# Two-layer hybrid decoder on 8 cores: attention values and softmax denominators from one full-width matmul

## The reference, cut to what matters

```python
DEPTH, D_MODEL, N_HEADS, KV_HEADS, HEAD_DIM, WINDOW = 2, 2048, 16, 4, 64, 128
def _layer(x, ...):
    z = x @ w_in                       # q 1024, k 256, v 256, conv 3*512, pool 512
    # A: sliding-window attention: query blocks of 128, 256 keys each, 4 query heads per kv head
    s = q @ k^T * HEAD_DIM**-0.5 + bias(distance);  s = -1e30 outside the window
    m = max(max(s), sink)
    a = (exp(s - m) / (sum(exp(s - m)) + exp(sink - m))) @ v
    # B: gated short convolution      c = gb * conv3(gc * h)
    # C: multi-scale causal pooling   pm = (trailing mean - token) @ pool_w * pool_scale
    x = LN(alpha * x + concat(a, c, pm) @ w_o)
    x = LN(alpha * x + (silu(g) * val) @ w_down)   # g, val from conv3(x @ w_up)
```

## Time and profile before

| | us |
|---|---|
| median of 3 runs | 2840.01 |
| all three | 2839.45, 2840.01, 2842.6 |
| the profiled execution, its own time | 2839.04 |
| its span, slowest core (2) | 2837.5 |
| spans of cores 0 to 7 | 2835.9, 2828.8, 2837.5, 2834.1, 2837.0, 2832.3, 2833.8, 2829.4 |
| granted TensorE clock, mean of a core | 0.987 to 0.990 |

### The profile page before, as it was taken

The page is one execution under the profiler, slowest core; times in us unless marked ns, Lnnn a source line. Parts: engine busy times, 40 slices in busy tenths (PEclk is TensorE's granted clock), DMA queues, the critical chain, the costliest instruction groups (busy, mean ns, idle before and its releaser), DMA issues.

```text
span 2837.5 us, 52754 instructions; the slowest of 8 cores (2828.8 to 2837.5 us)
## 1 busy us (share of the span) xinstructions
PE 2729.5 (96%) x18484; PEld 1739.9 (61%) x18484; DVE 1476.1 (52%) x3278; ACT 931.4 (33%) x2005; POOL 496.2 (17%) x755
## 2 busy tenths in 40 slices
PE   7999999999999999999999989999999999999994
PEld 4655666666666666665665556566666666666653
DVE  0375466563555355445616644775535544563546
ACT  1565055330232033113636630643203311330236
POOL 2221063000000000001623102610000000000024
PEclk9999999999999999999999999999999999999997
DMA  9515524434444443443472154344454344434425
GB/s 163 104 31 157 109 49 79 81 77 80 76 74 69 82 75 69 67 89 62 106 192 42 37 157 94 60 75 75 80 88 75 69 68 85 73 61 82 75 46 125
DMA packets 84349, 238.12 MB, mean 84 GB/s; under 512 B 9288, under 2 KB 30032, under 8 KB 83536
## 3 DMA queue, kind: packets, MB, share of 16 engines
q0 software_dynamic: 61136, 190.23, 38.6%
q1 hardware_dynamic: 22944, 44.41, 5.1%
HBM read 405.99 MB, written 21.27 MB: 151 GB/s over the span
## 4 chain that ended last, share of the span: by engine, by line
PE 93%; DVE 2%; ACT 2%; issue 1%; DMA 1%; POOL 1%; DVEq 0%; POOLq 0%; ACTq 0%
PE ps L196 93%; DVE xT L196 1%; DMA X<-xg 1%; ACT xT L196 1%; DVE scr L196 1%; ACT scr L196 0%; POOL xT L196 0%; ACT rstd L196 0%; DMA slab<-w_in 0%; DVE H L196 0%; POOL H L196 0%; DVE rstd L196 0%; ACT ps L196 0%; DVE small L196 0%; DVEq L191 0%
## 5 line engine op out<-in xcount | busy, mean ns | idle before, releaser
L196 PE MATMUL ps<-X,slab 128*128 128x386 bf16 (+3 forms) x10944 | 1681.7, 315 | 21.8 <-DMA slab<-w_in 11.8
L196 PEld LDWEIGHTS ps<-X,slab 128*128 128x128 bf16 x10944 | 1059.4, 97 | 628.1 <-issue 52.2
L196 PE MATMUL ps<-H,slab 128*128 128x384 bf16 (+1 forms) x5760 | 895.5, 314 | 0.0
L196 DVE SCALAR_TENSOR_TENSOR scr<-ps,fcw_s,scr 128x384 f32<-128x384 f32 (+1 forms) x1056 | 616.0, 584 | 410.7 <-ACT scr L196 353.9
L196 PEld LDWEIGHTS ps<-H,slab 128*128 128x128 bf16 x5760 | 561.6, 98 | 307.8 <-issue 7.1
L196 ACT ACTIVATE scr<-ps,fcw_s 128x384 f32<-128x384 f32 (+1 forms) x528 | 291.1, 553 | 1054.9 <-PE ps L196 1054.7
L196 DVE TENSOR_TENSOR xT<-xT,ps 128x384 f32<-128x384 f32 (+1 forms) x549 | 264.5, 521 | 207.8 <-PE ps L196 189.9
L196 POOL DMA_DIRECT2D slab<-w_up x176 | 93.6, 532 | 924.7 <-PE ps L196 924.7
L196 DVE TENSOR_TENSOR H<-scr 128x384 bf16<-128x384 f32 (+3 forms) x278 | 143.4, 518 | 98.1 <-ACT scr L196 69.6
L196 ACT ACTIVATE scr<-xT 128x384 bf16<-128x384 f32 (+1 forms) x192 | 94.5, 496 | 226.0 <-DVE xT L196 181.9
L196 DVE SCALAR_TENSOR_TENSOR xT<-xT,lna_s,ps 128x384 f32<-128x384 f32 x144 | 83.8, 583 | 139.6 <-PE ps L196 139.6
(11 more groups left out here) (111 smaller groups left out, 858.5 us busy)
## 6 DMA issues: line engine op xcount, KB each, us to landing
slab<-w_up POOLq DMA_DIRECT2D x176, 512.0 KB, 6.6
slab<-w_dn POOLq DMA_DIRECT2D x96, 384.0 KB, 5.7
slab<-w_in POOLq DMA_DIRECT2D x56, 512.0 KB, 10.6
slab<-w_o POOLq DMA_DIRECT2D x32, 512.0 KB, 7.5
xT<-xr SPq DMA_DIRECT2D x16, 531.0 KB, 7.4
xT<-spill SPq DMA_DIRECT2D x16, 531.0 KB, 9.1
slab<-w_dl POOLq DMA_DIRECT2D x16, 512.0 KB, 6.6
spill<-xT SPq DMA_DIRECT2D x2, 3072.0 KB
```

The source lines that it names most:

```text
L196: bi = getattr(engobj, name)(*a_, **k_)
```

## The change

- `Vt` and `V0t` get a layout of [10 blocks, 2 kv pairs, 3, 64]: the values of kv head 2gp, 64 ones, the values of kv head 2gp+1. DVE writes the ones once a layer (`memset` over 20x64 columns); ACT's eviction of the values writes the outer two thirds; POOL's copy to `V0t` takes all 384 columns, and its zeroing of row 0 spares the ones. The first two blocks that this half doesn't use are no longer kept (`VB`).
- `pv` issues one matmul per `ab` and chunk, with the 128 columns `[values, ones]` (`ab` = 0) or `[ones, values]` (`ab` = 1) as stationary matrix. `ab` = 0 goes to bank 7 (values on partitions 0 to 63, denominators on 64 to 127), `ab` = 1 to bank 3 (denominators on 0 to 63, values on 64 to 127).
- The logarithm is taken in two operations of 64 partitions, each reading one half of a bank and writing the other half of `rden`; the exponential stays one operation. `pv_out` becomes two products of 64 partitions.
- The one row of the sample values is written by 8 small DMAs on SP's queue (two per sample) in place of 4.
- Two of the four overlaid scratch buffers go; the two `rstd` tiles, widened to 420 columns, take their place in the rotation, so there are 10 as before. `pst` moves to a tile of its own.

```diff
+            VB = 0 if half else 1
-            Vt = overlay([("V", b) for b in range(11)], [11, 256], BF16)
+            Vt = overlay([("V", b) for b in range(VB, LB + 1)], [10, 2, 3, 64], BF16)
...
-            NOV = 4
-            NSA = NSCR + NOV
+            NOV = 2
+            NSA = NSCR + NOV + 2
...
+            scra += [(rstd_t[i][:, :], ("rstd", i)) for i in range(2)]
...
-                            for bank, lap, lres in ((7, vt[0:kk, b, kv * 64:kv * 64 + 64], (vn, b)), (3, onerow[0:kk, 0:64], "onerow")):
-                                P.pe(lambda e, rap=rap, lap=lap, bank=bank, ab=ab, ch=ch: e.matmul(
-                                    PSB[bank][ab * 64:ab * 64 + 64, 0:4 * nq], lhsT=lap, rhs=rap, start=(ch == 0), stop=(ch == 1)),
-                                    reads=[lres, ("PT", u % 2, ab)], writes=[("ps", bank)])
-                    P.act(lambda e: e.activation(out=rden[:, 0:4 * nq], in_=PSB[3][:, 0:4 * nq], func=AF.Ln), reads=[("ps", 3)], writes=["rden"])
+                            lap = vt[0:kk, b - VB, gp, ab:ab + 2, :].rearrange("p t d -> p (t d)")
+                            P.pe(lambda e, rap=rap, lap=lap, bank=(7, 3)[ab], ch=ch: e.matmul(
+                                PSB[bank][:, 0:4 * nq], lhsT=lap, rhs=rap, start=(ch == 0), stop=(ch == 1)),
+                                reads=[(vn, b), ("PT", u % 2, ab)], writes=[("ps", (7, 3)[ab])])
+                    P.act(lambda e: e.activation(out=rden[0:64, 0:4 * nq], in_=PSB[7][64:128, 0:4 * nq], func=AF.Ln), reads=[("ps", 7)], writes=["rden"])
+                    P.act(lambda e: e.activation(out=rden[64:128, 0:4 * nq], in_=PSB[3][0:64, 0:4 * nq], func=AF.Ln), reads=[("ps", 3)], writes=["rden"])
                     P.act(lambda e: e.activation(out=rden[:, 0:4 * nq], in_=rden[:, 0:4 * nq], func=AF.Exp, scale=-1.0), reads=["rden"], writes=["rden"])
...
-                    P.dve(lambda e: e.tensor_tensor(out=H_t[:, 4 * gp:4 * gp + 4, q0 - BASE:q0 - BASE + nq],
...
+                    for ab in range(2):
+                        kb = 64 * ab
+                        bank = (7, 3)[ab]
+                        P.dve(lambda e, kb=kb, bank=bank: e.tensor_tensor(
+                            out=H_t[kb:kb + 64, 4 * gp:4 * gp + 4, q0 - BASE:q0 - BASE + nq],
...
+                    P.dve(lambda e: e.memset(Vt[:, :, :, 1, :], 1.0), writes=[("V", b) for b in range(VB, LB + 1)])
```

More of the change, by code:

```diff
@@ L362, in build @@
         rden = sb("rden", [128, 512])
-        rstd_t = [sb(f"rstd{i}", [128, 384]) for i in range(2)]
+        rstd_t = [sb(f"rstd{i}", [128, SCW]) for i in range(2)]
+        pst = sb("pst", [128, 4, 75])
         PSB = [st.enter_context(nc.psum_tensor(f"ps{i}", [128, 512], F32)) for i in range(8)]
@@ L408, in program @@
             onerow = overlay(["onerow"], [128], BF16)
-            V0t = overlay([("V0", b) for b in range(11)], [11, 256], BF16)
+            V0t = overlay([("V0", b) for b in range(VB, LB + 1)], [10, 2, 3, 64], BF16)
             dP = overlay(["dP"], [128], BF16)
             dPT = overlay(["dPT"], [64], BF16)
-            NOV = 4
-            NSA = NSCR + NOV
+            NOV = 2
+            NSA = NSCR + NOV + 2
             SCRA0 = ov["off"]
@@ L666, in pv_out @@
                     gp, q0, nq = units[u]
-                    P.dve(lambda e: e.tensor_tensor(out=H_t[:, 4 * gp:4 * gp + 4, q0 - BASE:q0 - BASE + nq],
-                                                    in0=PSB[7][:, 0:4 * nq].rearrange("p (j q) -> p j q", j=4),
-                                                    in1=rden[:, 0:4 * nq].rearrange("p (j q) -> p j q", j=4), op=ALU.mult),
-                          reads=[("ps", 7), "rden"], writes=[r for j in range(4) for r in Hr(4 * gp + j, q0, q0 + nq)])
+                    for ab in range(2):
[3 more added lines that the diff above has]
+                            out=H_t[kb:kb + 64, 4 * gp:4 * gp + 4, q0 - BASE:q0 - BASE + nq],
+                            in0=PSB[bank][kb:kb + 64, 0:4 * nq].rearrange("p (j q) -> p j q", j=4),
+                            in1=rden[kb:kb + 64, 0:4 * nq].rearrange("p (j q) -> p j q", j=4), op=ALU.mult),
+                            reads=[("ps", bank), "rden"], writes=[r for j in range(4) for r in Hr(4 * gp + j, q0, q0 + nq)])
                 for u in range(nu + 2):
@@ L1152, in layer @@
                 for s in range(NS):
-                    P.dma("sp", lambda e, s=s: e.dma_start(out=veff[0:1, s, :], in_=Vt[NP % 128 + s:NP % 128 + s + 1, LB, :]), reads=[("V", LB)], writes=[("veff", s)])
+                    for g in range(2):
+                        P.dma("sp", lambda e, s=s, g=g: e.dma_start(out=veff[0:1, s, g * 128:g * 128 + 128].rearrange("p (t d) -> p t d", t=2),
+                                                                    in_=Vt[NP % 128 + s:NP % 128 + s + 1, LB - VB, g, 0:3:2, :]),
+                              reads=[("V", LB)], writes=[("veff", s)])
                 side.append(attention(l))
```

10 lines of the change are left out of this document (5 added, 5 removed).

## The result

The changed kernel took 2855.49 us (median of 5 runs, 2849.02 to 2938.74), against 2840.01 before. The ratio is **1.0050 (95% interval 1.0037 to 1.0062)**; in a second series it was 1.0052 (1.0038 to 1.0066). The forecast was 2841.0 with a range up to 2849.0. The changed kernel is about 14 us slower: not within 0.2%, as forecast, but beyond it. (Some runs, such as that of 2938.74 us, are disturbed by a lower clock of a whole die; they are left out of every ratio here, and the cores of such a die out of every mean of cores.)

What follows compares the result with a forecast made beforehand. TensorE, busy 96% of the span, was taken to bound the kernel. 2839.04 - 4.8 (matmuls) + 5.9 (added ACT and DVE work) = 2840.1; the median lies 1.0 above that execution, so 2841.0 us, range 2834.5 to 2849.

Steps and rivals of the forecast that it cites:

- TensorE gains 4.8 us: Matmul groups of `pv`: four full-width streams replace eight paired half-width matmuls, saving shape changes; 5.6 less 0.8 us.
- I give them nothing: The 4 short units, switching between 128 and 34 rows at each chunk: no matmul saving counted.
- lengthens the wait: Six places where DVE works without a gap from before `pv` to the next wait: 0.8 us off TensorE's gain.
- Does half the height cost half the time?: Added logarithm and product: height is free, so each costs its full-height price, 587 and 686 ns.
- Eight places pay, together 5.9 us: Attention stages: added ACT and DVE work delays TensorE at eight places only, 5.1 of 5.9 us in layer 1.
- no idle time of the engine lies between it and TensorE's next wait: Test on 36 logarithms and 36 products: added work costs only where its engine has no idle time before TensorE's wait.
- The half clock: TensorE at 1.2 GHz: no term in the forecast; longer waits might bring it more often, 1 to 2 us each time.
- rival B: Layer 1 becomes bound by its helpers, DVE's product delaying all 18 units, 13.3 us there; 2849, chance 0.20.
- The rest at nothing: Memset of ones, POOL's wider copy, four more DMAs, scratch rotation and `pst`: no cost.
- The seams: Ends of the attention stages, 260 and 1662: about 2 us earlier and 1 us later than before.
- DVE would still be busy only 121 of 154 us: Argument against rival B: in layer 1's attention stage DVE would still not be full.

Runs made afterwards that it cites:

- the pair of kernels: Changed kernel with one full-height logarithm and product, with its four matmuls (wrong attention output) and with the old eight: 0.9984 and 1.0009 of before.
- the repeat: The changed kernel, unaltered, measured again in a second series against the kernel before: 1.0052.
- mm4_only: Changed kernel with its four matmuls but one full-height logarithm and product per unit (wrong attention output): 0.9984 of the kernel before when run again.
- mm4_both: mm4_only with logarithm and product each split into two half-height operations, logarithms from bank 3, products from bank 7: 1.0043 of the kernel before.
- new_split: Changed kernel with the second product moved behind the second transposes: 1.0052 of the kernel before.
- one_side: Kernel before with all eight half-width matmuls writing partitions 0 to 63, logarithm and product each in two halves (wrong output): 2863.8 us, one run.

## Why the prediction was wrong, point by point

**"TensorE gains 4.8 us": right in its mechanism, too small.** The trace gives 7.7 and the pair of kernels 7.3 to 7.5. The 32 long groups are as worked out (0.54 + 0.99 became 0.44 + 0.86 where a dense tile follows), 5.6 us. Missing are the four short units, "I give them nothing": there the eight matmuls took 0.94 us and the four take 0.49 (two units) and 0.65 (two), 1.5 in all; and another 0.9 is luck of the profiles, one group at 252 that ran at the half clock in the one and not in the other. That is 8.0, so of the 0.8 us that I took off because the saving "only lengthens the wait" at most 0.3 is there.

**"Does half the height cost half the time?" Answered with no: right.** 591 and 687 ns for 587 and 686.

**"Eight places pay, together 5.9 us": the step that failed.** TensorE's waits in the two stages of core 4 are 6.7 and 11.8 us before, 10.1 and 20.2 after: 11.8 more (0.7 of it put down to `issue`, no helper), and the two operations cost 16.2 us in the time. The eight places did pay, 8.3 together with what came shortly ahead of them (core 4, its times about 1 us earlier than in the earlier trace rows; the measured figure is the growth from start to start, the matmuls' saving left out):

| place before | forecast | measured |
|---|---|---|
| 227.5 | +0.74 | +0.86 |
| 1530.8 | +0.51 | +0.19, and +0.38 one dense tile ahead |
| 1556.0 | +1.21 | +1.27 |
| 1565.3 | +1.0 | +1.86 |
| 1600.3 | +0.89 | +0.1, and +1.1 four us ahead |
| 1622.9 | +0.31 | +1.0 |
| 1644.6 | +0.74 | +1.05 |
| 1650.0 | +0.47 | +0.49 |

The other 3.5 us lie in places that I had crossed off, like the two "ahead" in the table: above all at 252 (2.98 to 4.00), at 152 (0.45 to 1.80, of which 0.84 is taken from the next place), at 1616 (nothing to 0.60) and at 1636 (0.41 to 0.97). The fault is in the test that I put: "no idle time of the engine lies between it and TensorE's next wait". Idle time is no cover when the engine was idle because it waited for the other helper, which is late as well. The place ahead of 1600.3 shows it; the others were not followed up one by one. Timeline of the changed kernel, core 4:

```profile
1597.31 1.49 DVE L196 TENSOR_TENSOR H<-ps,rden 64x512 bf16<-64x512 f32 x2 [0.16 <-ACT rden L196]
...
1598.83 0.46 DVE L196 TENSOR_TENSOR xT<-scr,ps 128x294 f32<-128x294 f32 x1
...
1599.65 0.54 ACT L196 ACTIVATE xT<-xT,cw_s 128x290 f32<-128x290 f32 x1 [0.85 <-DVE xT L196]
...
1600.10 1.00 ACT L196 ACTIVATE xT<-ps 128x1024 bf16<-128x1024 bf16 x1
...
1601.24 0.61 PE L196 MATMUL ps<-ident_b,xT 128*128 128x128 bf16 x8 [0.95 <-ACT xT L196]
...
1605.31 0.61 PE L196 MATMUL ps<-ident_b,xT 128*128 128x128 bf16 x8 [2.27 <-DVE xT L196]
```

and of the kernel before, core 4, at the same place of the program:

```profile
1592.33 0.69 DVE L196 TENSOR_TENSOR H<-ps,rden 128x512 bf16<-128x512 f32 x1
...
1592.93 0.45 DVE L196 TENSOR_TENSOR xT<-scr,ps 128x294 f32<-128x294 f32 x1
...
1593.75 0.54 ACT L196 ACTIVATE xT<-xT,cw_s 128x290 f32<-128x290 f32 x1 [0.39 <-DVE xT L196]
...
1594.19 1.00 ACT L196 ACTIVATE xT<-ps 128x1024 bf16<-128x1024 bf16 x1
...
1595.34 0.61 PE L196 MATMUL ps<-ident_b,xT 128*128 128x128 bf16 x8
...
1599.45 0.61 PE L196 MATMUL ps<-ident_b,xT 128*128 128x128 bf16 x8 [2.19 <-DVE xT L196]
```

The two products take 1.49 us instead of 0.69 and push DVE's addition of the convolution; ACT, which had 0.39 us idle here, doesn't use that as cover: it now waits 0.85 for DVE, and only then copies the transposes of the *same* bank 6 that TensorE needs. The new wait of 0.95 is on ACT, four microseconds ahead of the wait on DVE that I had named, and that one grew by 0.08.

**The half clock: priced at nothing in the forecast, 1 to 2 us a time in rival B.** By the granted clock of cores 0, 2, 4 and 6, the profile of the result lost 6.6 us more to it than before, the repeat 11.7; each drop of 3.4 us costs 1.7. Here it can be seen in one stretch of layer 1, core 4, of before and of the repeat (the clock is the third figure from the end, 0.97 and 0.95); before:

```profile
1500.00:1680.00 180.00, 162.13 (x1283) 95.54 (x1283) 118.79 (x447) 113.44 (x242) 30.48 (x42) 0.97 0.31 80
```

the changed kernel, repeated:

```profile
1500.00:1680.00 180.00, 156.43 (x1153) 92.11 (x1163) 128.18 (x459) 124.97 (x263) 33.29 (x47) 0.95 0.27 59
```

With the waits the account is, for the profile of the result: +11.8 (waits) - 7.7 (matmuls) + 6.6 (clock) = +10.7, and the mean span of those cores is 10.4 longer; for the repeat, whose waits are 11.5 longer, +15.5 against 15.5. (The 0.9 us of half clock at 252 stands in two of the terms, so the account holds to about 1 us.) Of the clock's part, 2.6 us in either profile is the place behind the stage (here between 1815 and 1850), which comes with the layout and without a wait. In the two attention stages it is 4.3 and 7.7. That the added waits bring those is likely, since they stand in the stretches that have the waits, but no run changed the one without the other. How it comes about stays open.

**"The rest at nothing": half right.** The memset took 1.13 us twice and POOL's copy 0.51 for 0.40, and no wait in the stages grew by them; scratch and `pst` cost nothing. Yet the layout as a whole costs 4 us on the first half's cores, and all that its traces show for it is the half clock, 2.8 and 3.7 us.

**The seams.** I forecast the end of layer 0's stage 2 us earlier. On the same four cores the stage grew by 1.3 us in the profile of the result, and by 1.9 in the repeat. Layer 1's stage, forecast at +3 or so, grew by 7.8 and 9.2.

**Rival B** ("layer 1 becomes bound by its helpers", 2849, chance 0.20) was the nearest, 6 us under what was measured, and its price of 13.3 us for layer 1 is close to what the two operations cost there in the traces: 13.1 between mm4_only and mm4_both. But the mechanism that it names, DVE between product and reductions, is only part of it: new_split, which thins out exactly this queue, won nothing, and the logarithm cost as much as the product. I gave it too little since "DVE would still be busy only 121 of 154 us". It was busy 117.6, and TensorE waited all the same: here a chain through two helpers is late at 76% of either.

## What to carry to other kernels

These operations cost on half the partitions what they cost on all of them (591 and 687 ns for 587 and 686), so a layout that merges two matmuls and splits their eviction moves work from an engine that may have it cheap to two that don't. Before you call an operation hidden by its engine's idle time, look at who released the engine from that idle: if it is another helper that the change also loads, the time is no cover. And where TensorE waits at half of the units already, reckon with the whole price of what is added to the helpers rather than with that of the tight places, and with a few microseconds of half clock on top: the count gave 5.9 us, and the two operations cost 16. Before you read a difference of two such costs as an effect of one on the other, look at where the half clock falls in each kernel: here one place, far behind the stage, was worth 3 us to some of them and nothing to others.

## What was unexpected of the hardware

- Half-width matmuls that write different halves of the output partitions overlap even when the program has all four of the one half ahead of the four of the other: 0.99 us for eight. With all eight on one half it is 1.84. The Trainium skill (TensorE: Matmul & The Clock Gate, Part 3, What picks the tile position) has the start partition of the output pick the column tile, and the one_side trace agrees. Its strict order of starts (The mechanism) does not hold across the two halves here, by the 0.99: the first four, all on one half, would alone take four streams by the one_side trace, so the last four ran beside them.
- A group that is 0.85 us longer in each of 32 units lengthened the kernel by 10 us and not by 27, in one run: waits and clock gave back 18 of what TensorE had more to do.
- The half clock in the dense stage behind attention can move by some 3 us (0.9 to 3.4) with a change that adds no wait, on all four cores of one half and on two chips alike.
